# Pairs of half-array products in attention and index scores, and a forgetting sum in two single pass products

## The reference

```python
# block 1, sliding window attention: 16 heads of 64 channels, 4 key heads, window 128
scores = einsum('bnqhgd,bnkhd->bnhgqk', qb, kb) * (D ** -0.5)      # D = 64
scores = where(valid, scores, -inf)
probs = softmax(concatenate([scores, sink], -1))[..., :-1]
out = einsum('bnhgqk,bnkhd->bnqhgd', probs, vb)
# block 2, index scores that pick the keys: 16 heads of 64 channels, one key head
dots = einsum('bthd,bsd->bths', qi, k_idx) * (IDX_DIM ** -0.5)     # IDX_DIM = 64
score = einsum('bth,bths->bts', wi * (IDX_HEADS ** -0.5), relu(dots))
# block 2, attention with forgetting: 8 heads of 128 channels
cum = cumsum(log_f, axis=1)
logits = einsum('bthd,bshd->bhts', qb, k) * (HEAD_DIM ** -0.5) + (cum_q - cum_k)
```

## Time and profile before

| | |
|---|---|
| median of 3 runs | 2759.4 us (2756.27 to 2760.2) |
| profiled execution, its own time | 2753.84 us |
| its span | 2752.1 us |
| PE busy | 2691.9 us, 98% of the span |
| PEld busy | 2285.4 us, 83% |
| DVE busy | 1923.6 us, 70% |
| ACT busy | 1541.0 us, 56% |
| DMA | 493.20 MB, mean 179 GB/s |
| mean granted PE clock | 0.991 of full speed |

### The profile page before, as it was taken

How to read it: one execution, slowest core, us unless ns; L and a number is a source line. 1 busy time by engine, 2 the same in 40 slices (tenths; PEclk the granted TensorE clock), 3 DMA queues, 4 the chain that set the end, 5 groups by cost and what they waited for, 6 DMA issues and landing times.

```text
span 2752.1 us, 39728 instructions
## 1 busy us (share of the span) xinstructions
PE 2691.9 (98%) x14224; PEld 2285.4 (83%) x14224; DVE 1923.6 (70%) x3675; ACT 1541.0 (56%) x3037; POOL 17.0 (1%) x35
## 2 busy tenths in 40 slices
PE   8999999999999999999999999999999999999998
PEld 6778898888788888888887788887888888888886
DVE  6667777776677457756766678666678858876885
ACT  6565545555655445545556565545566646655664
POOL 0000000000000000000000000000000000000000
PEclk9999999999999999999999999999999999999999
DMA  7445455656566897666665554544656666666664
GB/s 255 130 137 153 153 159 156 223 186 221 162 196 188 176 199 206 186 196 185 191 192 160 176 151 153 172 145 129 200 163 196 188 190 192 190 190 192 186 191 154
DMA packets 136788, 493.20 MB, mean 179 GB/s; under 512 B 15680, under 2 KB 16192, under 8 KB 135824
## 3 DMA queue, kind: packets, MB, share of 16 engines
q1 hardware_dynamic: 134064, 480.11, 55.7%
q0 software_dynamic: 2240, 10.29, 3.1%
q10 hardware_dynamic: 288, 0.26, 0.0%
HBM read 486.41 MB, written 4.19 MB: 178 GB/s over the span
## 4 chain that ended last, share of the span: by engine, by line
PE 88%; DVE 4%; ACT 3%; DMA 3%; issue 1%; ACTq 0%; DVEq 0%
PE bank L572 87%; DMA raw<-in_ws_ffn 3%; DVE lo L1482 1%; ACT hi L993 1%; DVE X L1485 0%; DVE arena L1482 0%; PE bank L603 0%; DVE u_t L1482 0%; ACT sq_t L1080 0%; DVE arena L1485 0%; ACT arena L1327 0%; PE bank L660 0%; DVE arena L2067 0%; ACT L1327 0%; ACT arena L1043 0%
## 5 line engine op out<-in xcount | busy, mean ns | idle before, releaser
L1482 DVE TENSOR_TENSOR lo<-raw,hi 128x512 fp32r<-128x512 f32 x1804 | 1233.9, 690 | 776.9 <-ACT hi L993 694.1
L993 ACT CAST hi<-raw 128x512 fp32r<-128x512 f32 x1804 | 1106.8, 620 | 970.1 <-PE bank L572 888.5
L572 PE MATMUL bank<-XS,hi 128*128 128x512 f32 x4272 | 1181.3, 398 | 12.3 <-DVE XS L1485 5.8
L572 PEld LDWEIGHTS bank<-XS,hi 128*128 128x128 f32 x4272 | 732.7, 189 | 120.8 <-ACT hi L993 10.2
L572 PEld LDWEIGHTS bank<-XS,lo 128*128 128x128 f32 x4272 | 656.2, 189 | 91.9 <-DVE lo L1482 0.4
L572 PE MATMUL bank<-XS,lo 128*128 128x256 f32 x4272 | 681.2, 281 | 0.0
L572 PE MATMUL bank<-hi,HS 128*128 128x512 f32 x1696 | 473.7, 391 | 1.3 <-DVE u_t L1482 1.1
L572 PEld LDWEIGHTS bank<-hi,HS 128*128 128x128 f32 x1696 | 317.2, 188 | 67.5 <-issue 2.1
L572 PE MATMUL bank<-lo,HS 128*128 128x512 f32 x848 | 278.8, 390 | 0.0
L572 PE MATMUL bank<-hi,XS 128*128 128x512 f32 x960 | 274.8, 401 | 2.9 <-ACT hi L993 2.0
L572 PEld LDWEIGHTS bank<-hi,XS 128*128 128x128 f32 x960 | 179.8, 192 | 46.0 <-ACT hi L993 5.2
(11 more groups left out here) (180 smaller groups left out, 1129.9 us busy)
## 6 DMA issues: line engine op xcount, KB each, us to landing
raw<-in_ws_ffn SPq DMA_DIRECT2D x528, 512.0 KB, 3.6
raw<-in_ws_mix SPq DMA_DIRECT2D x338, 512.0 KB, 3.6
raw<-in_ws_ple SPq DMA_DIRECT2D x35, 512.0 KB, 4.2
arena<-in_gains POOLq DMA_DIRECT2D x4, 1024.0 KB, 8.0
arena<-in_xt SPq DMA_DIRECT2D x8, 256.0 KB, 6.1
X<-in_xt POOLq DMA_DIRECT2D x1, 2048.0 KB, 10.5
t5rows<-arena POOLq DMA_DIRECT2D x8, 256.0 KB, 11.4
out<-arena SPq DMA_DIRECT2D x8, 256.0 KB, 2.9
```

The costliest lines, as they stand in the source:

```text
L572: return eng.matmul(o, l, r, start=start, stop=stop, skip_group_check=True)
L993: eng.copy(hi[:, b % SPL, :], raw[:, u % RAW, part * BW:(part + 1) * BW]).then_inc(halved.next(b), 1)
L1482: return eng.tensor_tensor(o, a, b, op)
```

## The change

The products of two heads that lie on different halves of the array are issued in turn, and the index heads go two to a visit. For attention the second head of each unit must then read the other 64 partitions: the columns of `w_in` are reordered so that its queries lie there, and ACT makes a second copy of the turned keys with the halves swapped. The forgetting's sum is split in two float32r parts, held beside the identity's columns in a new buffer `picks`, and added by two float32r products. A constant that nothing read (`reset`, 256 columns) goes.

```diff
-    ("ident", 128), ("ones", 256), ("sw", 384), ("causal", 384), ("reset", 256), ("eps", 1), ("freq", 32)])
+    ("ident", 128), ("ones", 256), ("sw", 384), ("causal", 384), ("eps", 1), ("freq", 32)])
...
-            out["q", g, i] = sum((list(range(h, h + 64)) for h in (AQ + 64 * (4 * j + g) for j in (2 * i, 2 * i + 1))), [])
+            pair = (2 * i, 2 * i + 1) if g % 2 == 0 else (2 * i + 1, 2 * i)
+            out["q", g, i] = sum((list(range(h, h + 64)) for h in (AQ + 64 * (4 * j + g) for j in pair)), [])
...
+        picks = sb("picks", [P, 2 * T + 8], F32R)
+        a_over = region(HB + 3584, 512)
+        a_kb = [a_over[:, 256 * i:256 * i + 256] for i in range(2)]
+        b_cum, b_unit = picks[:, 0:2 * T], picks[:, 2 * T:]
@@ tensor, turn @@
-                    free[b] = [(laid, (g.g, k))]
+                    free[b] = [(laid, "over" if g.i == 0 else (g.g, k))]
@@ tensor, attention @@
-                    on.wait_ge(laid, (by["qkv", 0].g, 0))
+                    on.wait_ge(laid, "over")
-                    half = slice(64 * (j % 2), 64 * (j % 2) + 64)
                     for i in range(2):
-                        g = 2 * gp + i
                         clear(b[i])
-                        for q0, kn, o in queries:
-                            t = mm(bank[b[i]][:, o:o + kn], a_qa[g][j // 2][half, q0:q0 + P], a_ka[j // 2][half, 0:kn], True, True)
-                        t.then_inc(a_pe.next((x, "scores", i)), 1)
+                    for q0, kn, o in queries:
+                        for i, keys in enumerate((a_ka, a_kb)):
+                            row = 64 * ((j + i) % 2)
+                            half = slice(row, row + 64)
+                            t = mm(bank[b[i]][:, o:o + kn], a_qa[2 * gp + i][j // 2][half, q0:q0 + P], keys[j // 2][half, 0:kn], True, True)
+                            if q0:
+                                t.then_inc(a_pe.next((x, "scores", i)), 1)
@@ outputs: one loop over the heads becomes three @@
-                    for i in range(2):
-                        o = bank[b[0]][64 * i:64 * i + 64, 0:T]
-                        mm(o[:, 0:P], v0, a_pt[w][:, i, 0:P], True, True)
-                        mm(o[:, P:T], v0, a_pt[w][:, i, P:2 * P], True, False)
-                        t = mm(o[:, P:T], v1, a_pt[w][:, i, 2 * P:3 * P], False, True)
+                    o = [bank[b[0]][64 * i:64 * i + 64, 0:T] for i in range(2)]
+                    for i in range(2):
+                        mm(o[i][:, 0:P], v0, a_pt[w][:, i, 0:P], True, True)
+                    for i in range(2):
+                        mm(o[i][:, P:T], v0, a_pt[w][:, i, P:2 * P], True, False)
+                    for i in range(2):
+                        t = mm(o[i][:, P:T], v1, a_pt[w][:, i, 2 * P:3 * P], False, True)
@@ tensor, index @@
-                for h in range(16):
-                    if h:
-                        yield h * IDX_STEP
+                for c in range(8):
+                    if c:
+                        yield 2 * c * IDX_STEP
+                    pair = (2 * c, 2 * c + 1)
...
+                    for h in pair:
+                        clear(3 + h % 4)
                     for q0, kn, o in queries:
-                        t = mm(bank[k][:, o:o + kn], b_iq[half, c, q0:q0 + P], b_ki[half, 0:kn], True, True)
+                        for h in pair:
+                            half = slice(64 * (h % 2), 64 * (h % 2) + 64)
+                            t = mm(bank[3 + h % 4][:, o:o + kn], b_iq[half, c, q0:q0 + P], b_ki[half, 0:kn], True, True)
@@ tensor, forget @@
-                    on.wait_ge(m_dve, "cum")
+                    on.wait_ge(ready, "cum")
+                    pick = b_unit[96:104, h:h + 1].to_broadcast([8, P])
                     for q0, kn, o in queries:
                         mm(bank[b][:, o:o + kn], b_bq[:, h, q0:q0 + P], b_bk[:, h, 0:kn], True, False)
-                        t = mm(bank[b][:, o:o + kn], ident[96:104, 96 + h:97 + h].to_broadcast([8, P]),
-                               b_misc[96:104, 0:kn], False, True)
+                        for part in (0, T):
+                            t = mm(bank[b][:, o:o + kn], pick, b_cum[96:104, part:part + kn], False, part > 0)
@@ scalar, quarter_of_heads, keys only @@
+                    if g.i == 0:
+                        on.wait_ge(sines, "cos")
+                        eng.copy(a_over[0:64, :], src[64:128, :])
+                        eng.copy(a_over[64:128, :], src[0:64, :]).then_inc(laid.next("over"), 1)
@@ scalar, misc @@
+                yield d + 7
+                lanes = slice(96, 104)
+                on.wait_ge(m_dve, "cum")
+                eng.copy(b_unit[lanes, :], ident[lanes, 96:104])
+                eng.copy(b_cum[lanes, 0:T], b_misc[lanes, :]).then_inc(upper.next("cum"), 1)
@@ vector, misc @@
+                yield d + 8
+                lower(b_cum[lanes, :], b_misc[lanes, :], "cum")
```

More of the change, by code:

```diff
@@ L646, in attention @@
                     gp, j = x // 4, x % 4
-                    on.wait_ge(laid, (by["qkv", 0].g, 0))
+                    on.wait_ge(laid, "over")
                     on.wait_ge(laid, (by["qkv", 1 + gp].g, 1))
-                    half = slice(64 * (j % 2), 64 * (j % 2) + 64)
                     for i in range(2):
-                        g = 2 * gp + i
                         clear(b[i])
-                        for q0, kn, o in queries:
-                            t = mm(bank[b[i]][:, o:o + kn], a_qa[g][j // 2][half, q0:q0 + P], a_ka[j // 2][half, 0:kn], True, True)
-                        t.then_inc(a_pe.next((x, "scores", i)), 1)
+                    for q0, kn, o in queries:
+                        for i, keys in enumerate((a_ka, a_kb)):
+                            row = 64 * ((j + i) % 2)
+                            half = slice(row, row + 64)
+                            t = mm(bank[b[i]][:, o:o + kn], a_qa[2 * gp + i][j // 2][half, q0:q0 + P],
+                                   keys[j // 2][half, 0:kn], True, True)
+                            if q0:
+                                t.then_inc(a_pe.next((x, "scores", i)), 1)
                     yield at + 9
@@ L743, in index @@
             def index():
-                for h in range(16):
-                    if h:
-                        yield h * IDX_STEP
-                    c, half = h // 2, slice(64 * (h % 2), 64 * (h % 2) + 64)
-                    k = 3 + h % 4
+                for c in range(8):
+                    if c:
+                        yield 2 * c * IDX_STEP
+                    pair = (2 * c, 2 * c + 1)
                     on.wait_ge(scaled, by["iq", c].g)
                     on.wait_ge(m_dve, "ki")
-                    clear(k)
+                    for h in pair:
+                        clear(3 + h % 4)
                     for q0, kn, o in queries:
-                        t = mm(bank[k][:, o:o + kn], b_iq[half, c, q0:q0 + P], b_ki[half, 0:kn], True, True)
-                    t.then_inc(i_pe.next(h), 1)
-                    free[k] = [(i_act, h)]
+                        for h in pair:
+                            half = slice(64 * (h % 2), 64 * (h % 2) + 64)
+                            t = mm(bank[3 + h % 4][:, o:o + kn], b_iq[half, c, q0:q0 + P], b_ki[half, 0:kn], True, True)
+                            if q0:
+                                t.then_inc(i_pe.next(h), 1)
+                                free[3 + h % 4] = [(i_act, h)]
             def kv(g):
@@ L1027, in quarter_of_heads @@
                     on.wait_ge(a_pe, (g.g, k))
-                    eng.copy(o, bank[7 if g.i == 2 else 5 + k]).then_inc(laid.next((g.g, k)), 1)
+                    src = bank[7 if g.i == 2 else 5 + k]
+                    eng.copy(o, src).then_inc(laid.next((g.g, k)), 1)
+                    if g.i == 0:
+                        on.wait_ge(sines, "cos")
+                        eng.copy(a_over[0:64, :], src[64:128, :])
+                        eng.copy(a_over[64:128, :], src[0:64, :]).then_inc(laid.next("over"), 1)
             def quarter_of_values(g):
@@ L2366, in constants @@
     put("causal", np.concatenate([sw0, np.where(s <= t + P, 0.0, NEG)], 1))
-    put("reset", np.broadcast_to((np.arange(T) % 64 != 0).astype(np.float32), (P, T)))
     put("eps", EPS)
```

## The result

The changed kernel took 2740.55 us (median of 4 runs, 2736.28 to 2743.37), the kernel before 2757.84 us (4 runs, 2755.57 to 2760.2): 0.9936 of it, interval 0.9918 to 0.9954, or 17 us less. The forecast was 12.9 us less. The measured time lies at the low edge of the range given.

The account below looks back on a forecast made before the run. PE was taken as the bound, with 88% of the chain of waits. Gains 7.6 + 3.5 + 0.7 + 1.8 + 0.4 less 1.1 gave 12.9 us: 2759.4 to 2746.5 us, 8-in-10 range 2740.5 to 2754.5.

Parts of the forecast that it names:

- Overlap on row halves: Index and attention score visits: both heads' products run together on two row halves, the second head 0.11 us behind.
- Rival 1: Score visits: row halves don't overlap, so only merging index visits pays; 5.1 us gained, 2754.3 us; chance 0.13.
- Rival 2: Score visits: weight loads go one after another, 0.11 us each, visit 1.27 us; 8.4 us gained, 2751.0 us; chance 0.18.
- Rival 3: Score visits: each change of row half drains the array, 0.2 us; net 6.3 us slower, 2765.7 us; chance 0.05.
- Index: Index stage: sixteen visits become eight with both heads each; a pair saves 0.95 us, 7.6 us in all.
- Attention scores: Attention's eight score visits: 1.50 us becomes 0.96, 4.3 us saved, 80% taken because of PE's waits: 3.5 us.
- Outputs: Attention's output visits: interleaving saves 0.16 us a visit, about half of eight on the chain: 0.7 us.
- The forgetting's sum: Forgetting visits: two float32r products instead of one float32 save 0.22 us a head, 1.8 us; bounds −0.2 and 2.0.
- The clock: Low-clock stretches, about 1.7 us each: one more or fewer as likely, nothing in the sum, ±1.7 in the range.
- The copies of the keys: ACT near 59 us: two extra copies of 0.58 us delay DVE and PE, costing 1.1 us; bounds 0 and 2.8.
- The start: Kernel start: 256 columns fewer, 131 kB less to load at 320 GB/s, gain 0.4 us while the DMAs are full.
- Carrying the difference to the median: Whole kernel: the profiled execution was 5.6 us below the runs' median; that difference was added to the forecast.

Follow-up runs that it names:

- third experiment: The kernel before with attention's score products issued in turn for the two heads, both still on the same 64 partitions: 2755.32 us (1 run).
- second: The kernel before with eight two-head index visits, all products of the even head first, then all of the odd head: 2750.02 us, 0.998.
- last experiment: The changed kernel with attention's scores head after head, each head still on its own half: 2740.44 us (1 run).
- sixth: The changed kernel with attention's output products head after head again: 2745.34 us (1 run).
- all three edits: The changed kernel with later key copies from the arena, four index heads a visit and the forgetting's 8-row products last: 2734.35 us, 0.9917.

## Why the prediction was right in its main mechanism, and which steps failed

The overlap on the two halves came as forecast. Three steps failed:
- *The index stage's path.* "ACT and DVE keep their ticks", DVE stays below PE, and PE stays at 100%. The visits became shorter still than said (0.86 against 0.9 to 1.0), and PE then waited 0.77 us for DVE in that stage (58.23 of 59 us busy), which is the first thing the prediction itself named as a sign of being wrong. About 1.3 us of the visits' 8.3 were given back.
- *The size of attention's term*, 3.5 us, the largest error in the sum. It had the second head 0.11 us behind, where 0.007 was measured, and took off a fifth for PE's waits, of which nothing was found: 5.2 us.
- *The clock in the forgetting stage*, put at nothing: a stretch that cost 1.7 us went with the float32 products.

Term by term:

- **Overlap on row halves: right.** The visits have two records at once, 0.86 us for twice the products. Rival 1 (no overlap) holds only on one half, as the third experiment shows (1.50). Rival 2 (loads one after another) fell: the second pair of products starts at 213 and 220 ns, the third at 325 and 332, so two loads fit into 0.11 us where one after another they ask 0.22, and the visit is 0.86, not 1.27. Rival 3 (a drain at each change of half) fell: 1.6 or more was its mark. The step's size was off by the lag, 0.11 us forecast and 0.007 found. The order in turn, which the change was built on, is not what brings the overlap: head after head on two halves has it too (second and last experiments).
- **Index: 7.6 forecast, 7.0 found**, the same to 0.1 us in all nine profiled executions with two heads a visit. The visits save 8.3 rather than 7.6, and the sentence that DVE would stay below PE failed: on the average of the stage it does, but at single transposes PE now waits for it, 0.77 us at one. A mean of 42.2 of 62 us said nothing about these.
- **Attention scores: 3.5 forecast, 5.2 found.** The visits save 0.65 each, 5.2 in all. From 72 to 220 us the changed kernel gains 6.7 us on the one before (+1.92 to −4.80), of which the outputs are 1.1. The kernel with the outputs undone, whose only edit in this stretch is in the scores, gains 5.6. Both executions and that of before had the clock at its lower level for 10.2 us there, and one of the eight visits, which lay in it, saves 1.1 us (2.52 to 1.38) instead of 0.65. PE's waits for DVE in this stretch are the same in that kernel as before, to 0.1 us (3.5 ahead of line 660's transposes, 3.3 ahead of line 627's). So all that the visits save arrives, and the step that took off a fifth failed. The second execution of the change gains 9.7 there (+0.99 to −8.75), with only 3.4 us at the lower clock: the 6.8 us less at half speed are worth 3.4, which is the difference.
- **Outputs: 0.7 forecast, 1.1 found.** PE saves 0.27 a visit, not 0.16 (the lag again), and half of it arrives, as said. The other half shows as waits: PE's four largest waits for DVE in this stretch are each 0.3 us longer with the interleaved outputs than without (0.9, 2.1, 1.0 and 3.6 us against 0.6, 1.8, 0.7 and 3.3).
- **The forgetting's sum: 1.8 forecast, 2.0 found.** The 128-column product took 0.36 where 0.37 was worked out from the weight loads, that of 256 columns 0.42 for 0.44. Narrow products are not slower in this format.
- **The clock: nothing forecast, 1.7 found.** "One more or one fewer is as likely" failed. The stretch of the earlier trace rows stood right behind three forgetting visits, and it goes with the 8-row products of float32: it is there in six executions of six with them, in one of eight without. I had the row and took it for chance. Why these products would bring the low clock isn't shown, and one kernel, with one profiled execution, is all that isolates them. Over the whole program the clock gave nothing between the two profiled executions: the low stretches ahead of the one at the end sum to 41.0 us in both, since the one at the keys (next term) grew by as much as this one took away. So the forecast's net was right by luck, and its sign of being wrong, a sum that moves by more than two stretches, did not come.
- **The copies of the keys: 1.1 forecast, 1.8 to 2.4 found** between the batches at 60 and 72 us in the seven profiled executions that have them there (1.8 with the copies alone). It goes through ACT, DVE and PE as said, though at the earlier transposes. 1.3 of it is the wait, and the rest comes with the lengthened low stretch, which the forecast had named as a bound.
- **The start: 0.4 forecast, not measurable.** At 43 us the changed kernel's batches are 0.3 earlier than before. But kernels without this edit are 0.05 to 0.7 earlier there, and kernels with it lie between 1.7 earlier and 1.2 later.
- **Carrying the difference to the median: right in direction, too large.** The stretch from 220 to 1624 us was 3.8 us quicker in the profiled execution of before than in that of the change. But the 5.6 us came from a median of three runs. The median of the four set beside the change stands 4.0 above the profiled execution, and those of the 9 to 23 later runs 0.9 to 2.1 (2754.7 to 2755.96).

Two smaller slips: the 13.0 us that the prediction sets beside its 14.7 should read 12.9, its own sum, and 1690 to 1730 us is not where DVE is busiest (36.3 of 40 us there, 36.9 from 2050 to 2090).

The sum with measured terms is 7.0 + 5.2 + 1.1 + 2.0 + 1.7 − 1.8 = 15.2 us, where 12.9 was forecast. The two profiled executions differ by 15.1 when the 3.8 us of the second row of the table are set aside. The medians show 17.3 and, in a later set of runs, 16.6, with an interval of 12.7 to 22.6 around the first, which takes in the 12.9. So of the 4.4 us between forecast and measurement, 2.3 are named: attention's scores and the clock, 1.7 each, and 0.6 of the outputs and the sum, less 1.7 by which index, keys and start fell short. The other 2.1 are within what the runs can tell.

## What to carry to other kernels

In this kernel, products of 64 rows came at half price only if the two heads lay on different halves of the partitions. The order in which they are written did not matter with four records of the other head ahead, and cost 0.27 us a visit with six. A copy of the keys to the other half pays, and costs least where ACT is idle. Merging visits saves their edges as well, about 0.4 us for each visit fewer here (0.2 within the visit, 0.2 around it), until the engine that empties the banks is late. Before a mean load is taken to clear another engine, look at the wait that would come next at each place where PE depends on it.

## What was not expected of the hardware

- TensorE started products ahead of earlier ones in the program when their part of the array was free. With four records of the other half ahead the lag was 13 ns (second and last experiment), with six records ahead on the other column half 275 ns (sixth). In alternating order it was 7 ns. Whether the number of records sets this, or rows against columns, stays open.
- Weight loads for two halves went on at once: two of 128 columns within 0.11 us, the pace of single ones in the earlier trace rows.
- A stretch of 1.2 GHz followed 8-row products of float32 in the six profiled executions that have them. The new sum is free of it but once, in the kernel with these products last, and with the same order there is none in the version of all three edits; what decides that is open.
- At the keys, 1.3 us more waiting came with a low stretch of 6.8 us instead of 3.4, seven executions of seven with the copies at that place against none of seven without. That adds 0.5 to 1.0 us to the wait.
